# A second, residue-ordered pair of high and low parts of x for the first 512 value columns of a hybrid decoder layer

## The reference, cut to what matters

```python
proj = x @ w_in + b_in                       # x (512, 1024), w_in (1024, 6916)
qa, ka, va, qb, kb, vb, qc, kc, vc, fc, gates = split(proj)
# A: three groups of four heads, (window, dilation) = (128,1), (512,4), (2048,16)
# for dilation d, positions are split by residue mod d: token s + d*i goes to row i of sequence s
def strided(t):
    return t.reshape(B, L, dil, H, 64).transpose(0, 2, 1, 3, 4).reshape(B * dil, L, H, 64)
o_a = dilated_attention(qa * scale, ka, va, rel_bias)
...
x = layer_norm(alpha * x + mixer(x)); x = layer_norm(alpha * x + cross_attention(x)); x = layer_norm(alpha * x + swiglu(x))
```

## Time and profile before

| | |
|---|---|
| median of three runs | 854.13 us |
| the profiled execution's own time | 854.09 us |
| its span, first to last instruction | 852.3 us |
| TensorE busy | 99% |
| VectorE busy | 76% |
| ScalarE busy | 51% |
| GpSimd busy | 13% |
| mean granted TensorE clock | 0.999 |

### The profile page before, as it was taken

The page is one execution under the profiler, slowest core; times in us unless marked ns, Lnnn a source line. Parts: engine busy times, 40 slices in busy tenths (PEclk is TensorE's granted clock), DMA queues, the critical chain, the costliest instruction groups (busy, mean ns, idle before and its releaser), DMA issues.

```text
span 852.3 us, 14765 instructions
## 1 busy us (share of the span) xinstructions
PE 843.0 (99%) x5634; PEld 758.0 (89%) x5634; DVE 648.7 (76%) x1179; ACT 435.6 (51%) x911; POOL 110.1 (13%) x118
## 2 busy tenths in 40 slices
PE   9999999999999999999999999999999999999996
PEld 9999998877578999998889789899999999888785
DVE  5888667778566978786757688688998998877844
ACT  5455576158643555464424644465656665424521
POOL 5202000353200101100000010111111111000000
PEclk9999999999999999999999999999999999999999
DMA  9523633130013241426604111233333333651101
GB/s 300 165 89 119 156 110 124 50 100 2 1 50 103 97 148 51 148 65 233 223 25 157 45 47 51 99 100 100 100 100 104 117 119 109 255 190 49 50 26 74
DMA packets 73219, 90.52 MB, mean 106 GB/s; under 512 B 3554, under 2 KB 63734, under 8 KB 73150
## 3 DMA queue, kind: packets, MB, share of 16 engines
q1 hardware_dynamic: 72766, 89.15, 31.5%
q0 software_dynamic: 384, 0.43, 0.4%
HBM read 87.05 MB, written 2.52 MB: 105 GB/s over the span
## 4 chain that ended last, share of the span: by engine, by line
PE 49%; DVE 1%; issue 1%; ACT 0%; DVEq 0%; POOLq 0%; POOL 0%; ACTq 0%
PE ps L3645 7%; PE ps L3644 7%; PE ps L3643 7%; PE ps L3017 7%; PE ps L3019 7%; PE ps L3018 7%; PE ps L3701 1%; PE ps L3703 1%; PE ps L3702 1%; PE ps L3054 1%; PE ps L3197 1%; PE ps L3274 0%; PE ps L3234 0%; PE ps L3586 0%; DVE w_lo L2895 0%
## 5 line engine op out<-in xcount | busy, mean ns | idle before, releaser
L3645 PE MATMUL ps<-xt_lo,w_hi 128*128 128x256 f32 x288 | 81.5, 283 | 0.0
L3644 PE MATMUL ps<-xt_hi,w_lo 128*128 128x256 f32 x288 | 81.5, 283 | 0.0
L3643 PE MATMUL ps<-xt_hi,w_hi 128*128 128x256 f32 x288 | 81.5, 283 | 0.0
L2027 DVE TENSOR_TENSOR w_lo<-raw,w_hi 128x1024 fp32r<-128x1024 f32 (+1 forms) x42 | 50.4, 1202 | 39.2 <-ACT w_hi L1378 39.1
L1378 ACT CAST w_hi<-raw 128x1024 fp32r<-128x1024 f32 (+1 forms) x42 | 43.0, 1029 | 63.7 <-PE ps L3019 52.1
L3017 PE MATMUL ps<-xt_hi,w_hi 128*128 128x512 f32 (+1 forms) x160 | 62.0, 388 | 0.0
L3019 PE MATMUL ps<-xt_lo,w_hi 128*128 128x512 f32 (+1 forms) x160 | 61.5, 384 | 0.0
L3018 PE MATMUL ps<-xt_hi,w_lo 128*128 128x512 f32 (+1 forms) x160 | 61.4, 384 | 0.0
L3136 PE MATMUL ps<-xt_hi,w_hi 128*128 128x256 f32 x216 | 61.2, 283 | 0.0
L3643 PE MATMUL ps<-s_hi,w_hi 128*128 128x256 f32 x216 | 61.1, 283 | 0.0
L3644 PE MATMUL ps<-s_hi,w_lo 128*128 128x256 f32 x216 | 61.1, 283 | 0.0
(11 more groups left out here) (456 smaller groups left out, 2675.8 us busy)
## 6 DMA issues: line engine op xcount, KB each, us to landing
raw<-in_w_ffn_in SPq DMA_DIRECT2D x36, 512.0 KB, 4.3
raw<-in_w_in SPq DMA_DIRECT2D x31, 512.0 KB, 3.8
raw<-in_w_in SPq DMA_DIRECT2D x9, 1024.0 KB, 5.0
raw<-in_w_ffn_out SPq DMA_DIRECT2D x7, 1024.0 KB, 4.8
raw<-in_w_mix_out SPq DMA_DIRECT2D x4, 1024.0 KB, 4.8
raw<-in_w_ffn_in SPq DMA_DIRECT2D x4, 1024.0 KB, 5.3
out_w<-in_w_ffn_out SPq DMA_DIRECT2D x4, 1024.0 KB, 8.6
resid<-in_x SPq DMA_DIRECT2D x2, 1024.0 KB, 8.8
```

The costliest lines, as they stand in the source:

```text
L2027: dve.tensor_tensor(lo, src, f32(hi), ALU.subtract).then_inc(lo_done, pieces_counted(p))
L3643: pe.matmul(dst, w_h[:, k, :], x_h[:, k, :], start=clear and k == 0, stop=False, skip_group_check=True)
L3644: pe.matmul(dst, w_l[:, k, :], x_h[:, k, :], start=False, stop=False, skip_group_check=True)
L3645: ins = pe.matmul(dst, w_h[:, k, :], x_l[:, k, :], start=False, stop=k == 3, skip_group_check=True)
```

## The change

A second pair of parts of x, `xr_hi` and `xr_lo`, holds the tokens sorted by residue. It is written from `xt_raw` by new instructions, `residue_split(k)` on ScalarE and `residue_rest(k)` on VectorE, which read every fourth float and write adjacent ones. The 96 matmuls of the 512 value columns read this pair with `natural`, and `residue` is gone. The pair lies over space of q, k and value tiles, which are written later. `x_split` and `x_rest` stay, behind the residue forms and the weight's split; TensorE waits for all eight `x_rest` before the first 256 value columns. One pair of counts, `residue_mem_hi` and `residue_mem_lo`, serves the new parts and the parts of `mem`, which used to have a pair of their own.

Moved: on ScalarE split(PV0 + 1) from behind the fourth cast of a sum to behind the second; on VectorE rest_of(PV0) from behind the fourth sum to behind the third, sum rests 1 and 2 from ahead of the drain of the 512 columns to behind rest_of(PV0 + 1), sum rests 3 and 4 into the first head block, and the drain of the 256 columns from behind P6's rest to behind the block's last difference of weights.

```diff
--- before.py
+++ after.py
@@ -494,6 +494,10 @@
         with ExitStack() as st:
+            xr_hi = sb("xr_hi", [P, KT, SEQ], F32R, st)
+            sb("hold_xr", [P, T_N * SEQ - KT * SEQ], F32, st)
+            xr_lo = sb("xr_lo", [P, KT, SEQ], F32R, st)
+        with ExitStack() as st:
             sb("hold_qk", [P, T_N * SEQ + TT * 768 + TT * VBC_N + LINE_PAD], F32, st)
...
@@ -591,7 +595,7 @@
         turned, turn_hi, turn_lo = sem("turned"), sem("turn_hi"), sem("turn_lo")
-        mem_hi, mem_lo = sem("mem_hi"), sem("mem_lo")
+        residue_mem_hi, residue_mem_lo = sem("residue_mem_hi"), sem("residue_mem_lo")
         seg_ps, seg_ready, seg_out, table_in = sem("seg_ps"), sem("seg_ready"), sem("seg_out"), sem("table_in")
...
@@ -1103,7 +1107,7 @@
                     sp.wait_ge(seg_out, 16 * 4)
-                    sp.wait_ge(mem_lo, 4)
+                    sp.wait_ge(residue_mem_lo, KT + 4)
                     tables(tab1, rows1, 0, N_AH, SEG1, 256)
...
@@ -1390,9 +1394,14 @@
 
+            def residue_split(k):
+
+                act.wait_ge(x_in[k if k < 4 else k // 2 + 2], 16)
+                act.copy(xr_hi[:, k, :].rearrange("p (s i) -> p s i", s=4),
+                         xt_raw[:, k, :].rearrange("p (i s) -> p s i", s=4)).then_inc(residue_mem_hi, 1)
+
             def x_split(k):
 
-                act.wait_ge(x_in[k if k < 4 else k // 2 + 2], 16)
                 act.copy(xt_hi[:, k, :], xt_raw[:, k, :]).then_inc(turn_hi, 1)
...
@@ -1452,14 +1461,19 @@
             for k in range(4):
+                residue_split(k)
+                first_split(k)
                 x_split(k)
-                first_split(k)
+            residue_split(4)
+            residue_split(5)
+            split(2)
             x_split(4)
             x_split(5)
-            split(2)
+            residue_split(6)
+            residue_split(7)
+            split(3)
             x_split(6)
             x_split(7)
-            split(3)
             def gate_round(kind, n):
...
@@ -1550,7 +1564,7 @@
                         ks = slice(2 * block_no(n), 2 * block_no(n) + 2)
-                        act.copy(memt_hi[:, ks, :], memt_raw[:, ks, :]).then_inc(mem_hi, 1)
+                        act.copy(memt_hi[:, ks, :], memt_raw[:, ks, :]).then_inc(residue_mem_hi, 1)
                 gate_round("P3", -2)
...
@@ -1572,7 +1586,8 @@
                 act.copy(head_sum(j, 0), HEAD_SUMS[j - 1]).then_inc(gx_hi, 1)
-            split(PV0 + 1)
+                if j == 2:
+                    split(PV0 + 1)
             head_blocks()
...
@@ -2040,6 +2055,13 @@
 
+            def residue_rest(k):
+
+                dve.wait_ge(residue_mem_hi, k + 1)
+                dve.tensor_tensor(xr_lo[:, k, :].rearrange("p (s i) -> p s i", s=4),
+                                  xt_raw[:, k, :].rearrange("p (i s) -> p s i", s=4),
+                                  f32(xr_hi[:, k, :]).rearrange("p (s i) -> p s i", s=4), ALU.subtract).then_inc(residue_mem_lo, 1)
+
             def x_rest(k):
...
@@ -2181,14 +2203,19 @@
             for k in range(4):
+                residue_rest(k)
+                first_rest(k)
                 x_rest(k)
-                first_rest(k)
+            residue_rest(4)
+            residue_rest(5)
+            rest_of(2)
             x_rest(4)
             x_rest(5)
-            rest_of(2)
+            residue_rest(6)
+            residue_rest(7)
+            rest_of(3)
             x_rest(6)
             x_rest(7)
-            rest_of(3)
 
...
@@ -2243,7 +2270,7 @@
                 gate_op_rest("P6", -N_HEAD_BLOCK)
-                drain_piece(PV0 + 1)
+                head_sum_rest(3)
                 for n in range(-N_HEAD_BLOCK, -1):
...
@@ -2254,19 +2281,23 @@
                     gate_t4(n)
-                    if not first:
+                    if first:
+                        drain_piece(PV0 + 1)
+                    else:
                         gate_c12(n - 1)
                     gate_op_rest("P1", n + 1)
+                    if first:
+                        head_sum_rest(4)
                     gate_op_rest("P4", n)
...
                     if n < 4 - N_HEAD_BLOCK:
-                        dve.wait_ge(mem_hi, block_no(n) + 1)
+                        dve.wait_ge(residue_mem_hi, KT + block_no(n) + 1)
                         ks = slice(2 * block_no(n), 2 * block_no(n) + 2)
                         dve.tensor_tensor(memt_lo[:, ks, :], memt_raw[:, ks, :], f32(memt_hi[:, ks, :]),
-                                          ALU.subtract).then_inc(mem_lo, 1)
+                                          ALU.subtract).then_inc(residue_mem_lo, 1)
                 gate_t23(-1)
...
@@ -2284,6 +2315,11 @@
 
+            def head_sum_rest(j):
+
+                dve.wait_ge(gx_hi, j)
+                dve.tensor_tensor(head_sum(j, 1), HEAD_SUMS[j - 1], f32(head_sum(j, 0)), ALU.subtract).then_inc(gx_lo, 1)
+
             def small_tables():
...
@@ -2298,20 +2334,16 @@
             dve.tensor_tensor(A_11, A_22, A_11, ALU.subtract).then_inc(gx_sum, 1)
+            rest_of(PV0)
             dve.wait_ge(gx_sum, 3)
...
             dve.tensor_scalar(bias_q, bias_t[:, 0:6], SCALE, None, ALU.mult).then_inc(gx_whole, 1)
-            rest_of(PV0)
-            for j in (1, 2):
-                dve.wait_ge(gx_hi, j)
-                dve.tensor_tensor(head_sum(j, 1), HEAD_SUMS[j - 1], f32(head_sum(j, 0)), ALU.subtract).then_inc(gx_lo, 1)
             drain_piece(PV12 + 3)
             rest_of(PV0 + 1)
+            for j in (1, 2):
+                head_sum_rest(j)
             small_tables()
-            for j in (3, 4):
-                dve.wait_ge(gx_hi, j)
-                dve.tensor_tensor(head_sum(j, 1), HEAD_SUMS[j - 1], f32(head_sum(j, 0)), ALU.subtract).then_inc(gx_lo, 1)
             head_blocks()
...
@@ -3032,8 +3064,6 @@
 
-            def residue(x, k, s):
-                return x[:, k, s:s + 4 * (P - 1) + 1:4]
 
...
@@ -3068,27 +3098,28 @@
                 pe.wait_ge((first_hi, hi_done)[k % 2], k // 2 + 1)
-                pe.wait_ge(turn_hi, k + 1)
+                pe.wait_ge(residue_mem_hi, k + 1)
                 for t in range(TT):
-                    pe.matmul(ps[:, 2 + t, :], residue(xt_hi, k, t), w_hi[1 - k // 2][:, w], start=k == 0, stop=False)
-                pe.wait_ge(turn_lo, k + 1)
+                    pe.matmul(ps[:, 2 + t, :], natural(xr_hi, k, t), w_hi[1 - k // 2][:, w], start=k == 0, stop=False)
+                pe.wait_ge(residue_mem_lo, k + 1)
                 for t in range(TT):
-                    pe.matmul(ps[:, 2 + t, :], residue(xt_lo, k, t), w_hi[1 - k // 2][:, w], start=False, stop=False)
+                    pe.matmul(ps[:, 2 + t, :], natural(xr_lo, k, t), w_hi[1 - k // 2][:, w], start=False, stop=False)
                 pe.wait_ge((first_lo, lo_done)[k % 2], k // 2 + 1)
                 for t in range(TT):
-                    ins = pe.matmul(ps[:, 2 + t, :], residue(xt_hi, k, t), w_lo[1 - k // 2][:, w], start=False, stop=False)
+                    ins = pe.matmul(ps[:, 2 + t, :], natural(xr_hi, k, t), w_lo[1 - k // 2][:, w], start=False, stop=False)
                 if k % 2:
...
                 pe.wait_ge(lo_done, p + 1)
-                pe.wait_ge(turn_lo, 2 * p + 2)
-                v_piece(p, 2 * p, 2, 512, lambda t: (2 + t, 0, 0, 0), residue)
+                pe.wait_ge(residue_mem_lo, 2 * p + 2)
+                v_piece(p, 2 * p, 2, 512, lambda t: (2 + t, 0, 0, 0), natural, xr_hi, xr_lo)
 
...
                       stop=True).then_inc(seg_ps, 1)
+            pe.wait_ge(turn_lo, KT)
             for p in range(PV0, PQA):
...
@@ -3497,7 +3528,7 @@
 
-            pe.wait_ge(mem_lo, 4)
+            pe.wait_ge(residue_mem_lo, KT + 4)
             pe.wait_ge(turn_lo, 2 * TT + 2)
...
                 pe.wait_ge(lo_done, PKX + n + 1)
```

## The result

The changed kernel takes 855.12 us, the median of 22 runs (854.50 to 856.19), against 854.08 for 22 runs of the kernel before: a ratio of 1.0013, 95% interval [1.0007, 1.0018]. It is 1.0 us slower, within the 0.2% that the prediction called "the same", and 1.8 us from the predicted 853.35: the sign is wrong and the range (852.5 to 855.0) is missed by 0.1. The profiled execution has a span of 853.3 us (before: 852.3).

The account below looks back on a forecast made before the run. TensorE, busy 843.0 of 852.3 us, was taken to bound the kernel. From 854.09, minus 0.78 for closer starts, plus 0 for the new work, came 853.31, predicted as 853.35 for the median; range 852.5 to 855.0.

Parts of the forecast that it names:

- Term 1: The 96 matmuls of the 512 value columns start closer together with adjacent loads: gain 0.78 us, bounds 0 and 1.0.
- Term 2: New strided casts on ScalarE and subtractions on VectorE in the opening take 0.62 and 0.69 us, off TensorE's path: 0 us.
- Rival A: Strided reads cost ScalarE 1.02 and VectorE 1.14 us, TensorE waits before piece 2: 854.8 us; chance 0.14 with its half form.
- GpSimd's bound: Before the table matmul, five GpSimd steps may each lengthen by 1 us, ending at 25.9 us, wanted at 27.6.
- Term 3: The moved sum rests, drain and weight steps up to the first head block keep TensorE's dates; no cost counted.
- P4's margin: In the first head block, P4's rest ends at 47.8 us, wanted by TensorE at 48.1: 0.3 us of slack.

Follow-up runs that it names:

- the loads alone: The kernel before, with the 96 matmuls of the 512 value columns loading adjacent floats, sorting left out: 853.33 us, ratio 0.9993.
- the kernel with one pause: The changed kernel with VectorE waiting for GpSimd's first table cast ahead of its strided subtraction for block 6: 854.60 us, ratio 1.0007.
- the last version: The changed kernel without a sorted copy for k = 0, natural parts 1 to 7 and table matmuls later, value weight rests earlier: 853.75 us, ratio 0.9996.
- the filled pause: The kernel before with two more adjacent subtractions on VectorE, into a scratch tile, between x_rest(7) and rest_of(3): 854.38 us, one run.
- the later table matmuls: The changed kernel with TensorE's two table matmuls and their waits behind the first piece of the 256 value columns: 854.17 us, ratio 1.0003.

## Why the prediction was wrong

- **Term 1 held**: loads of 188 ns, starts 0.227 us apart, 0.64 us at the table matmul with the loads alone (0.78 was forecast; the first start lay 0.08 us later there).
- **Term 2 failed, in its price.** I took 0.62 and 0.69 us for the strided forms; they measure 1.11 and 1.05. The wrong step is the reading of the earlier trace rows: a strided 0.694 us was called "the time of any subtraction", though the same line's adjacent form took 0.482. Within one line the stride had cost 1.44 times, and that ratio on 0.69 gives 1.0, about what was measured (the line has one input where the subtraction has two, so the closeness may be chance). The ScalarE row beside it read PSUM and said nothing of SBUF. The Trainium skill's rule (Advanced Engine Details and Errata, SBUF Cachelines), that an access going to another 16-byte line with each element pays, was right on all three engines; I had set VectorE's row against it and should have read it as support.
- **Rival A was the mechanism, not its size.** It put the first start 0.4 later and piece 2 at 18.2; the trace has 0.32 and 17.45. Its sum used durations (1.14) where a row of subtractions follows at distances of 1.0 (11.97, 12.96). By itself it came to 0.35 - 0.26 = +0.1, not +0.7: its 854.8 lies near the measured 855.1 only because the larger share, GpSimd's 0.90, which no case of mine had, fills the difference.
- **GpSimd's bound failed.** "Five earlier steps may each lengthen by 1 us, from 20.9 to 25.9" took the longest VectorE instruction as the longest hold. One cast was held 6.03 us, over eight instructions, and ended at 22.99 instead of 17.36; with the five steps behind it, which took 6.3 us instead of 3.5, the last ended at 29.3. The forecast's own cover, VectorE's pauses, was what the price of term 2 took away.
- **Term 3 held**: the moves cost nothing, and P4's margin, forecast at 0.3, is 0.57 us: its rest ends at 49.36, wanted at 41.29 + 6 x 1.44 = 49.93. It is the next limit all the same: in the kernel with one pause and in the last version TensorE came for it 0.2 us early.

## What to carry to other kernels

Moving a stride from TensorE's load to the engines that prepare the operand pays only if those engines' rows have that much air: price the strided form from the same line's adjacent form, and add it up over the row, not per instruction. Before filling the last pauses of VectorE, list what GpSimd does beside it and who waits for that, since small GpSimd steps can be held through the whole row and not only through one instruction.

## What the runs showed of the hardware

- Reading SBUF at a step of 16 bytes cost on three engines: a load of 128x128 went from 188 to 310 ns, ScalarE's cast of 128x512 from 0.62 to 1.11 us, VectorE's subtraction from 0.68 to 1.05. Writing each float 512 bytes from the one before cost ScalarE's cast as much, 1.09 to 1.20 us.
- A GpSimd cast of 96x20 took 0.20 us in a pause of VectorE (17.74 us in the kernel before), up to 1.2 where it ended with one VectorE instruction, and 5.7 to 7.0 where it was held through a row. The Trainium skill (SBUF — State Buffer, Who interferes with whom) says that a VectorE instruction with two SBUF inputs and a GpSimd instruction that reads SBUF exclude each other, one blocked until the other's end. The traces agree that one blocks, but here the block lasted over eight instructions, not one. Why it ended with single instructions in other stretches without a pause (16.15 to 17.46 with the filled pause, 18.66 to 20.7 with one pause) stays open.
- The first four 128x512 matmuls took 1.25 to 2.09 us from execution to execution, at a granted clock of 1.00 in every one; what sets it stayed open. Where piece 2 waits for VectorE, this is absorbed: with the later table matmuls they took 1.31 us and in the changed kernel 2.08, and piece 2 starts at 17.45 in both.
